# Conditioning weights in blocks of two rows and 2048 columns, in place of eight rows and 512 columns

## The reference, cut to what matters

```python
def ada_chunks(cond, w, b):
    m = jax.nn.silu(cond) @ w + b          # (1024) @ (1024, 6144), once per layer and conditioning vector
    return jnp.split(m, 6, axis=-1)        # shift, scale, gate; shift, scale, gate

for layer in range(DEPTH):                 # DEPTH = 2
    sh1, sc1, g1, sh2, sc2, g2 = ada_chunks(cond, ada_w[layer], ada_b[layer])
    h = modulate(x, norm1_g[layer], sh1, sc1)      # rmsnorm(x) * (1 + sc1) + sh1
    # layer 0: h @ na_w_in -> attention and Fourier mixing -> @ na_w_out
    # layer 1: h @ sg_w_in -> chunked spatial gating -> @ sg_w_out
    x = x + g1 * mix
    h = modulate(x, norm2_g[layer], sh2, sc2)
    x = x + g2 * moe(h, router_w, router_b, ...)   # 16 experts, top 2
```

## Time and profile before

| | us |
|---|---|
| median of 3 runs | 1049.81 (1049.44 to 1052.66) |
| span of the profiled execution | 1049.3 |
| PE busy | 984.0 (94%) |
| conditioning products (L1742), PE busy in the groups of the page | 39.0 in the ring blocks alone |
| idle of PE before them, ended by a weight's landing | 24.4 |

### The profile page before, as it was taken

One profiled execution on the slowest core, in us unless ns is written; L12 is line 12 of the kernel. 1 busy time (PEld: TensorE's weight loads), 2 busy tenths in 40 slices (PEclk: granted clock), 3 DMA queues, 4 the chain that ended last, 5 costly groups with the idle time before them and its releaser, 6 DMA issues.

```text
span 1049.3 us, 13649 instructions
## 1 busy us (share of the span) xinstructions
PE 984.0 (94%) x5466; PEld 502.5 (48%) x5466; DVE 410.2 (39%) x940; ACT 179.0 (17%) x379; POOL 139.7 (13%) x149
## 2 busy tenths in 40 slices
PE   2799999999979999999999789999999999999997
PEld 1555545466554555544334244444555555444432
DVE  0210340013672657642333450350136666522336
ACT  4211100004661010111111151000121011111100
POOL 4100150001770000100100400010000001100003
PEclk9899999999799998899999989999999999999999
DMA  9989648965706105789998731320060037999977
GB/s 333 377 292 331 237 172 282 383 220 168 202 22 230 41 21 216 270 324 423 421 411 357 279 106 55 136 81 0 1 250 39 24 149 273 358 418 423 421 286 299
DMA packets 86405, 244.73 MB, mean 233 GB/s; under 512 B 7376, under 2 KB 22384, under 8 KB 73920
## 3 DMA queue, kind: packets, MB, share of 16 engines
q1 hardware_dynamic: 57952, 199.04, 49.2%
q0 software_dynamic: 8528, 27.99, 7.2%
q10 hardware_dynamic: 19856, 16.76, 5.1%
HBM read 215.66 MB, written 27.33 MB: 232 GB/s over the span
## 4 chain that ended last, share of the span: by engine, by line
PE 82%; DMA 8%; DVE 4%; issue 2%; POOL 2%; ACT 2%; SPq 0%; POOLq 0%; DVEq 0%; ACTq 0%
PE bank L1772 25%; PE bank L1906 14%; PE bank L1784 14%; PE bank L1920 7%; DMA ring<-in_ada_w 4%; PE bank L1728 4%; PE bank L1742 4%; PE bank L1813 2%; PE bank L1897 2%; DMA ring<-in_moe_w_up 2%; PE bank L2088 1%; PE bank L1798 1%; PE bank L2163 1%; POOL h_feat L892 1%; PE bank L2080 1%
## 5 line engine op out<-in xcount | busy, mean ns | idle before, releaser
L1772 PE MATMUL bank<-ring,h_feat 128*128 128x512 f32 x640 | 282.3, 599 | 3.7 <-issue 2.7
L1772 PEld LDWEIGHTS bank<-ring,h_feat 128*128 128x128 f32 x640 | 120.9, 192 | 151.3 <-issue 150.0
L1906 PE MATMUL bank<-ring,uv 128*32 128x512 f32 (+2 forms) x592 | 144.6, 614 | 2.7 <-ACT uv L975 2.1
L1784 PE MATMUL bank<-ring,h_feat 128*128 128x512 f32 x320 | 146.9, 609 | 0.0
L1784 PEld LDWEIGHTS bank<-ring,h_feat 128*128 128x128 f32 x320 | 59.9, 194 | 65.4 <-issue 65.3
L1906 PEld LDWEIGHTS bank<-ring,uv 128*32 128x32 f32 (+2 forms) x592 | 46.6, 131 | 71.8 <-issue 67.6
L1920 PE MATMUL bank<-ring,uv 128*32 128x512 f32 (+2 forms) x296 | 72.7, 596 | 1.3 <-issue 0.7
L1742 PE MATMUL bank<-ring,small 128*2 128x128 f32 x1152 | 39.0, 291 | 24.4 <-DMA ring<-in_ada_w 24.4
L1491 DVE TENSOR_TENSOR uv<-uv,bank 128x256 f32<-128x256 f32 x25 | 10.5, 421 | 130.7 <-ACT uv L983 130.7
L1906 PE MATMUL bank<-bz,uv 128*64 128x512 f32 (+1 forms) x112 | 49.4, 594 | 0.0
L865 POOL DMA_INDIRECT uv<-h_rows,small x23 | 21.8, 947 | 200.0 <-PE bank L1897 161.4
(11 more groups left out here) (241 smaller groups left out, 1114.5 us busy)
## 6 DMA issues: line engine op xcount, KB each, us to landing
ring<-in_ada_w SPq DMA_DIRECT2D x16, 2048.0 KB, 13.9
ring<-in_moe_w_gate SPq DMA_DIRECT2D x20, 1024.0 KB, 12.7
ring<-in_moe_w_up SPq DMA_DIRECT2D x20, 1024.0 KB, 14.9
ring<-in_moe_w_down SPq DMA_DIRECT2D x20, 1024.0 KB, 16.2
h_tok<-in_moe_w_down SPq DMA_DIRECT2D x12, 1024.0 KB, 16.0
y_rows<-uv SPq DMA_DIRECT2D x23, 512.0 KB, 16.0
ring<-in_na_w_in SPq DMA_DIRECT2D x4, 2048.0 KB, 16.1
bz<-in_ada_w SPq DMA_DIRECT2D x4, 2048.0 KB, 12.1
```

Source lines behind the costliest of these rows:

```text
L1772: last = mm(jbank(key)[:, :], HT[:, cc, P * t:P * (t + 1)], w[:, cc, :], start=cc == 0, stop=cc == DC - 1)
L1784: last = mm(jbank(key)[:, :], HT[:, cc, P * t:P * (t + 1)], blk_ap(("out", layer, b))[:, cc, :], start=cc == 0, stop=cc == DC - 1)
L1906: last = mm(bank[2][32 * q:32 * (q + n), :], XT[:, b, cc, 32 * q:32 * (q + n)], w[:, :, cc, :], start=cc == 0, stop=cc == DC - 1)
```

## The change

The block is turned: in place of 8 rows per partition with 512 columns, a block now has 2 rows per partition (rows 8p+2b and 8p+2b+1) with all 2048 columns of the group. It is 2 MB as before, in 256 pieces of 8 KB in place of 1024 pieces of 2 KB, and takes the same places and semaphores. PE multiplies a block as 2 steps of rows with 4 column tiles, each a stationary operand of 128 x 2 against 512 columns. The 512 columns of tile j are four runs of 128, one from each 512, so each PSUM value ends in the same place as before. The sum over rows now runs over the four blocks of a group in one PSUM bank, whose accumulation starts in the group's first block and ends in its last.

```diff
         def split_half(i):
-            return (PS[:, 0:2048], RING[:, 16384:18432])[i].rearrange("p (c n) -> p c n", c=4)
-
-        def ada_chunk(layer, b, cc):
+            return (PS[:, 0:2048], RING[:, 16384:18432])[i]
+
+        def ada_row(layer, b, i):
             s, _ = place[("ada", layer, b)]
-            return split_half(cc // 4)[:, cc % 4, :] if s == SPLIT else block(s)[:, cc, :]
+            row = split_half(i) if s == SPLIT else block(s).rearrange("p c n -> p (c n)")[:, 2048 * i:2048 * i + 2048]
+            return row.rearrange("p (u j n) -> p j u n", u=4, j=4)
...
-        ada_v = ada_w.rearrange("l (p c) (g u n) -> l g u p c n", c=DC, u=4, n=512)
+        ada_v = ada_w.rearrange("l (p b i) (g n) -> l g b p i n", b=4, i=2, n=4 * 512)
...
-                        sp.dma_start(split_half(i), w[:, 4 * i:4 * i + 4, :]).then_inc(block_in[s], 16)
+                        sp.dma_start(split_half(i), w[:, i, :]).then_inc(block_in[s], 16)
                 else:
-                    sp.dma_start(block(s), w).then_inc(block_in[s], 16)
+                    sp.dma_start(block(s).rearrange("p c n -> p (c n)").rearrange("p (i n) -> p i n", i=2), w)\
+                        .then_inc(block_in[s], 16)
...
-                for cc in range(DC):
-                    w = ada_chunk(layer, b, cc)
+                for i in range(2):
+                    w, cc = ada_row(layer, b, i), 2 * (b % 4) + i
                     for j in range(4):
-                        last = mm(out[32 * j:32 * j + 2, P * (b % 4):P * (b % 4) + P], scond[:, :, cc],
-                                  w[:, P * j:P * (j + 1)], start=cc == 0, stop=cc == DC - 1)
+                        last = mm(out[32 * j:32 * j + 2, :], scond[:, :, cc], w[:, j], start=cc == 0, stop=cc == DC - 1)
```

## The result

Over 14 runs of each, the changed kernel takes 1054.39 us (1051.07 to 1058.01) and the one before 1050.05 (1044.62 to 1052.66). The ratio is 1.0046, interval 1.003 to 1.0062: slower by 4.8 us, 3.2 to 6.5. The forecast was 1050.6 and no change. The profiled execution took 1057.15, 2.8 over its kernel's median, so its span of 1055.4 overstates the loss. I read differences at marks: the start of the same instruction in both profiles. Two marks serve throughout: the first projection product, and the last conditioning block (the 24th), behind which the change touches nothing.

A forecast was written before the change was run, and what follows sets the result against it. PE bounds the kernel (busy 984.0 of 1049.3 us), with waits for weights. Start +2.6, 193 us -1.3 and products -0.5 make +0.8, 1050.1 on the profiled span; median predicted 1050.6 us, range 1045.8 to 1054.2.

The forecast's parts named there:

- The products: PE's 20 conditioning blocks on the chain: wide products take 0.025 us less per block, -0.5 us in all; bounds -2.8 to 0.
- 193 us: PE's idle 1.31 us before a block not yet landed: faster loads bring two blocks 1.0 earlier, wait goes, -1.3 us.
- Turns: SP's and ACT's queues alternate packet by packet; beside 8 KB packets a 4 KB turn costs 0.449 us, a 64-byte one 0.32.
- Rival (1): Queues share more by bytes, x keeps its pace, start 2 to 3 us earlier: -4.3, 1045.5 us; chance 0.17.
- x: Load of x on ACT's queue at the start: its turns done at 19.7 us in place of about 12.2.
- ACT's hold: ACT stands behind its own issues until 65.5 queue turns pass; first sum of squares at 23.4 us, not 13.75.
- From there on: Start after ACT's release: normalized at 34.1 us, transposes 4.0, block 3's product ends at 40.5, not 37.9: +2.6 us.
- Block 2's landing: Weights at the start: block 2's turns end at about 25.6 us, not 27.3, landing 2.7 later; PE then idles some 3.
- Rival (2): Small transfers' lag from turn to landing triples, landing at 44, DVE 3.4 later: +4.2, 1054.0 us; chance 0.21.
- The signs I had listed: Profile after: ACT starts near 23 us, L1213 near 40 before finishing, transposes await ACT, no wait at 193, blocks near 1.8.
- my upper bound (+5.6): Worst case for the start: ACT's release and DVE's wait for small transfers both 3 us worse, +5.6 us.

## Why the prediction was wrong

No change was forecast, and it is slower by 0.46%. The mechanism was the forecast's own, with one term too small: the time for which ACT is held by its own issues.

- **The products:** right. A block by itself takes 1.83 in the chain of after and 1.86 before, predicted 1.84. The four strips hold.
- **193 us:** the wait is gone and the gain of 1.3 right, but in part by luck. The faster loads do take it away (with the old start, where nothing else has moved, no wait is left), and so does the late start by itself, with pieces of 2 KB. The changed blocks in pieces of 2 KB leave 0.16 of it, and I can't say why. With the products the gain behind the start is 1.75 in the profile and 2.3 in the timed kernel with the old start; predicted 1.8.
- **Turns:** right. One piece a turn, 0.457 us for a turn of x (7.0 x 16 / 245; predicted 0.449) and 0.308 (0.32). Rival (1) falls with it. The rule of the Trainium skill named beside it ("DMA: Bandwidth & Descriptors", Queues, rings and completion order) does not describe these queues: 443 to 442 is one to one.
- **x:** 1.05 late. Turn 54 of ACT's queue came at 20.75, predicted 19.7. I had named the reason: 298 / 16 = 18.6 turns were done by 5.0, not 21.3, as the first 8 KB packet came at 4.0.
- **ACT's hold, the step that failed:** "before the last tiny vector it is 152 and 65.5, 87 left". I took it as what the queue accepts and put ACT's release at turn 65.5. It came at turn 1204 / 16 = 75.3, with 152 - 75.3 = 77 left. The other two holds agree: 119 - 676 / 16 = 77 left at 15.73, and 137 - 1013 / 16 = 74 at 23.67. Turn 65 passed at 24.26, and ten more turns at 0.3 make the first sum of squares 27.25. So of the 3.85 between 23.4 and 27.25 x is about 1 and the lower count 2.8.
- **From there on:** right. Normalized at 37.95 (predicted 34.1, +3.85); transposes 4.41 (4.0), block 3's product 1.90 (2.4); finished at 44.4 (40.5, +3.9). The start costs 6.5 in place of 2.6. With 3.9 more the sum of the forecast reads +4.7 in place of +0.8; timed +4.8 (3.2 to 6.5), so that close a match is more than the measurement can tell. The low clock's share is no constant: in two other profiles with the same start the transposes took 3.76 and 3.90, after 10.58 of waiting in place of 9.12.
- **Block 2's landing:** put at 28.3 (its turns to end at 25.6, and 2.7 to the landing). Its turns ended near 24.8 and it landed at 25.55. So PE stood 9.12 before the transposes, where I had some 3. ACT came last, so this cost at most the 0.4 by which the transposes were slower than put.
- **Rival (2):** its time was near (1054.0, timed 1054.39), its mechanism was not at work. The small transfers landed at 39.08, predicted 39.9, 5.4 before PE had block 3, and taking DVE's wait away moved nothing. Its premise, that the time from turn to landing grows with the packets, fails: for block 2 it fell from 2.7 to 0.8.
- **The signs I had listed:** the first sum of squares was to start near 23; it starts at 27.25. L1215 was to stand directly before the finishing; it stands 5.4 earlier. The others came: the transposes led by a wait for ACT, x's last landing near 21, PE's landing waits mostly at block 0 (12.91 of 18.4), no wait at 193 us, and blocks at 1.8.

The error that mattered is one of reasoning: I had two readings of the hold, 82 and 87, both beside packets of 2 KB, and took them for a constant, while the change multiplied the price of each turn of it by 3.3. The 3 us that my upper bound (+5.6) allowed for a later ACT was short of the 3.85. The trace before had more readings than I used, on the other queue: SP's issue of its third block is held for 9.52 us and let go with 148 - 814 / 16 = 97 pieces left, its projection block for 5.68 with 278 - 3167 / 16 = 80 left. That is no constant either.

**Open:** what sets the count. When an issue that had been held for over 1 us was let go, the pieces per DMA engine that were issued before it and not yet moved were 82 and 87 in the kernel before, 80 and 85 with the changed rows in 2 KB, 78 and 77 with 4 KB, 77, 74 and 75 with 8 KB, and 88 where the weights waited for x and the queue ran alone. ACT's queue up to 6.5 us in that kernel:

```profile
q10 hardware_dynamic: 504, 1.41, 61.1%
```

119 - 504 / 16 = 87.5. The issues behind it in that kernel took their usual 0.5 to 0.6 us with up to 147 - 785 / 16 = 98 left. More are left the faster the queue moves. A fixed delay between a piece's move and the room that it makes would give the reverse. No run varied the count by itself, so I name no mechanism. Open too is why the kernel before loses by the late transfers.

## What to carry to other kernels

Queues that share the DMA engines took turns piece by piece here, so a load in larger pieces made every turn of the other queue dearer (0.093 to 0.308 us from 2 KB to 8 KB), while a queue of 8 KB pieces moved 425 GB/s in place of 387. Before making a load's pieces larger, count the small pieces that another queue has to get through beside it, and what stands behind them. ACT, which issued more pieces than its queue took at once, was held itself, arithmetic and all. Let such an engine issue what is not needed soon behind its arithmetic, and put the wait for it late as well. The change and that move together gave 0.994 and 0.9949 of the time before, where the one gave 1.0046 and the other 1.0026.

## What the runs showed of the hardware that I had not expected

- An issue blocked its engine for 11.14 us. The count of pieces outstanding when a held issue was let go was no constant: 74 to 88 on ACT's queue, and 80 and 97 in two readings on SP's.
- One piece a turn held at every pair of sizes seen: 952 to 948 (2 KB, 64 bytes), 244 to 245 (8 KB, 4 KB), 443 to 442 (8 KB, 64 bytes and less).
- Which size of piece is best depended on what was held. With the hold, 2 KB and 4 KB (0.9977 and 0.9965, not told apart) beat 8 KB (1.0046); without it 8 KB (0.994 and 0.9949) beat 4 KB (0.9973).
- Two profiles of one kernel differed by 3.1 us between the same two marks (41.06 to 315.26, and 41.30 to 312.40), while from the first of these to the last conditioning block they agreed to 0.01. The gain of the 20 later blocks, some 2 us, can be read at a mark before 240 us and not at one behind it.
